# Softmax of differential attention: the maxima of both score maps by one vector instruction

## What is computed

```python
def diff_attend(q, keys, values, mask, lam):
    s = jnp.concatenate([jnp.einsum("bqhmd,bkhmd->bhmqk", q, k, preferred_element_type=jnp.float32)
                         for k in keys], axis=-1) * (B_HD ** -0.5)
    s = jnp.where(mask, s, jnp.finfo(jnp.float32).min)
    p = jax.nn.softmax(s, axis=-1)
    a = p[:, :, 0] - lam * p[:, :, 1]
    ...
    return sum(jnp.einsum("bhqk,bkhe->bqhe", a_i, v_i.astype(jnp.float32))
               for a_i, v_i in zip(parts, values))
```

## Time and profile before

| | |
|---|---|
| median of 3 runs | 3868.49 us (3865.95 to 3873.62) |
| profiled execution, its own time | 3872.43 us |
| its span, first to last instruction | 3870.3 us |
| PE busy | 3542.8 us (92%) |
| DVE busy | 1532.7 us (40%) |
| ACT busy | 1100.9 us (28%) |
| POOL busy | 787.7 us (20%) |

### The profile page before, as it was taken

One profiled execution on the slowest core, in us unless ns is written; L12 is line 12 of the kernel. 1 busy time (PEld: TensorE's weight loads), 2 busy tenths in 40 slices (PEclk: granted clock), 3 DMA queues, 4 the chain that ended last, 5 costly groups with the idle time before them and its releaser, 6 DMA issues. The chain is left out here.

```text
span 3870.3 us, 56244 instructions
## 1 busy us (share of the span) xinstructions
PE 3542.8 (92%) x21831; PEld 3369.7 (87%) x21831; DVE 1532.7 (40%) x2332; ACT 1100.9 (28%) x1863; POOL 787.7 (20%) x477
## 2 busy tenths in 40 slices
PE   5888888888897899999999998888898999999998
PEld 5888788788787899999999877777777999999998
DVE  2544534534433542222223344444445622222222
ACT  2332333332332221111112334434444221111111
POOL 1213313213212131111111311111110231111110
PEclk7999899899898899999999989999999999999999
DMA  2010000001000111111111111111111111111111
GB/s 87 17 29 18 24 27 19 24 18 28 24 18 18 39 44 44 45 44 45 44 44 44 59 46 51 51 51 51 51 50 34 44 44 46 44 48 43 46 44 63
DMA packets 254676, 155.75 MB, mean 40 GB/s; under 512 B 9521, under 2 KB 251587, under 8 KB 254403
## 3 DMA queue, kind: packets, MB, share of 16 engines
q1 hardware_dynamic: 254426, 152.14, 13.5%
HBM read 133.69 MB, written 18.42 MB: 39 GB/s over the span
## 5 line engine op out<-in xcount | busy, mean ns | idle before, releaser
L210 PE MATMUL ps<-x_hi,w_hi 128*128 128x364 f32 x2880 | 693.3, 349 | 30.6 <-DVE conv_in_sample L1090 17.5
L210 PE MATMUL ps<-x_hi,w_lo 128*128 128x364 f32 x2880 | 644.6, 332 | 0.0
L210 PE MATMUL ps<-x_lo,w_hi 128*128 128x364 f32 x2880 | 644.4, 332 | 0.0
L210 PEld LDWEIGHTS ps<-x_hi,w_hi 128*128 128x128 f32 x2880 | 502.6, 192 | 68.1 <-issue 21.5
L210 PEld LDWEIGHTS ps<-x_lo,w_hi 128*128 128x128 f32 x2880 | 509.5, 191 | 0.0
L210 PEld LDWEIGHTS ps<-x_hi,w_lo 128*128 128x128 f32 x2880 | 509.1, 191 | 0.0
L200 DVE TENSOR_TENSOR w_lo<-w_raw,w_hi 128x1024 fp32r<-128x1024 f32 x200 | 282.8, 1414 | 509.3 <-ACT w_hi L196 509.2
L196 ACT ACTIVATE w_hi<-w_raw 128x1024 fp32r<-128x1024 f32 x200 | 211.7, 1059 | 833.7 <-PE ps L210 616.0
L190 POOL TENSOR_TENSOR w_raw<-w_raw,params 128x1024 f32<-128x1024 f32 x120 | 232.9, 1944 | 891.0 <-DMA w_raw<-in_w_in_a 408.1
L210 PE MATMUL ps<-hidden_hi,w_lo 128*128 128x364 f32 x1536 | 338.3, 328 | 0.0
L210 PE MATMUL ps<-hidden_lo,w_hi 128*128 128x364 f32 x1536 | 337.7, 328 | 0.0
(11 more groups left out here) (321 smaller groups left out, 4967.0 us busy)
## 6 DMA issues: line engine op xcount, KB each, us to landing
w_raw<-in_w_up SPq DMA_DIRECT2D x64, 512.0 KB, 3.9
w_raw<-in_w_down SPq DMA_DIRECT2D x64, 512.0 KB, 3.4
w_raw<-in_w_in_a SPq DMA_DIRECT2D x32, 512.0 KB, 4.1
w_raw<-in_w_kv SPq DMA_DIRECT2D x16, 512.0 KB, 4.0
cache_pages<-in_cache_k SPq DMA_DIRECT2D x128, 64.0 KB, 1.9
cache_pages<-in_cache_v SPq DMA_DIRECT2D x128, 64.0 KB, 1.9
x_in<-in_x_prompt SPq DMA_DIRECT2D x8, 512.0 KB, 4.3
state_sample<-in_state_delta SPq DMA_DIRECT2D x8, 512.0 KB, 4.0
```

What stands on the lines that cost most here:

```text
L210: mm = nc.tensor.matmul(PS[:, bank + g, 0:GRP], wt, x[:, k, g * GRP:(g + 1) * GRP], start=(k == 0 and t == 0), stop=(k == chunks - 1 and t ...
```

## The change

One reduce now takes the maxima of both maps: it reads a view of PSUM with two rows per partition (`score_rows`) and writes two numbers, and one instruction negates both. The exponentials remain two instructions, and each waits for the joint maximum. The scores give one signal for a step, after the last mask matmul, where each map had its own. So that the two rows lie at an even distance, the short steps (0 to 3) put their maps in banks 0 and 1 or 2 and 3, where they had 0 and 2 or 1 and 3; the long steps keep their banks.

```diff
-    b_s = Steps(nc, "scores", 2 * NT)
-    b_mx = Steps(nc, "score_max", 4 * NT)
+    b_s = Steps(nc, "scores", NT)
+    b_mx = Steps(nc, "score_max", 2 * NT)
...
     def score_bank(i, m):
-        return 2 * m + (i % 2 if i < 4 else 0)
+        return 2 * (i % 2) + m if i < 4 else 2 * m
...
+    def score_rows(i):
+        b = score_bank(i, 0)
+        return PS[:, b:b + 2, 0:(i + 1) * P] if i < 4 else \
+            PS[:, 0:4, :].rearrange("p (m b) c -> p m (b c)", m=2)[:, :, 0:(i + 1) * P]
...
                 mm = nc.tensor.matmul(PS[:, score_bank(i, m) + i // 4, d], IDH[map_rows(m), part, :],
                                       MDH[map_rows(m), part, :], start=False, stop=part == 1)
-                if part == 1:
-                    mm.then_inc(b_s.sem, 1)
+        mm.then_inc(b_s.sem, 1)
...
                 for m in range(2):
-                    act.wait_ge(b_mx.sem, b_mx.at(h, 4 * i + 2 * m + 2))
+                    act.wait_ge(b_mx.sem, b_mx.at(h, 2 * i + 2))
...
             def maxima(i):
-                for m in range(2):
-                    dve.wait_ge(b_s.sem, b_s.at(h, 2 * i + m + 1))
-                    nc.vector.tensor_reduce(SC[:, i, 0, m:m + 1], score_row(i, m), AX.X, ALU.max).then_inc(b_mx.sem, 1)
-                    dve.wait_ge(b_mx.sem, b_mx.at(h, 4 * i + 2 * m + 1))
-                    nc.vector.tensor_scalar(SC[:, i, 1, m:m + 1], SC[:, i, 0, m:m + 1], -1.0, None, ALU.mult
-                                            ).then_inc(b_mx.sem, 1)
+                dve.wait_ge(b_s.sem, b_s.at(h, i + 1))
+                nc.vector.tensor_reduce(SC[:, i, 0, :], score_rows(i), AX.X, ALU.max).then_inc(b_mx.sem, 1)
+                dve.wait_ge(b_mx.sem, b_mx.at(h, 2 * i + 1))
+                nc.vector.tensor_scalar(SC[:, i, 1, :], SC[:, i, 0, :], -1.0, None, ALU.mult).then_inc(b_mx.sem, 1)
```

## The result

The change makes the kernel slower: 3920.86 us median (3918.33 to 3924.78, 4 runs) where the kernel before, run beside it, took 3868.08 (3865.95 to 3873.62, 4 runs). The ratio is 1.0135, 95% interval [1.0118, 1.0153], or +52.8 us. The forecast was 3903 in a range up to 3918: the direction was right, and the time lies 3 us above the upper end. The profiled execution took 3918.33 with a span of 3916.2, which is 45.9 us above the span of before.

A forecast was written before the change was run, and what follows sets the result against it. Bound: each softmax step's ring of VectorE, ScalarE and PE, without slack, delaying PE and the end. Lost overlap 30.7 + joint score signal 0.8 + POOL holds 3 = 34.5 us on 3868.5, giving 3903; range 3893 to 3918.

The forecast's parts named there:

- The lost cover: Softmax steps 1 to 7: map 0's exp no longer overlaps map 1's maximum; one exp lost less fixed costs, 30.7 us.
- The rivals that said not slower: VectorE's instructions bound (3850, chance 0.03); delay absorbed by PE or load (3868, 0.04); two-row maximum at one row's price (3864, 0.03).
- The holds: POOL's weight-slab scaling (L190) in the softmax loops holds VectorE's instructions in more heads than three: +3 us, bounds -5 and +8.
- the mix that the prediction names: Head 2's VectorE mix at 2449.31, expected to slide 1.4 us to 2450.7, behind POOL's scaling start at 2450.63.
- The upper bound of +8: Upper bound for added delay from POOL's slab scaling: all seven heads with such a slab are held.
- The one signal of the scores: First maximum also waits for map 1's last mask matmul, step 1 above all: 0.8 us, bounds 0 and 2.
- the banks: Steps alternate between two PSUM bank pairs as before, with PE's order and waits the same: nothing.
- PE's clock: Longer gaps before the scores may bring the lower granted clock to six more heads: 8.5 us, 3912, chance 0.20.
- the projection stretches stay unchanged: Sign of being right: softmax stretches grow some 4 to 6 us a head, while projections behind them keep their length.
- the rival: More than the sum: PE's lower clock at step 6 in six more heads, 6 x 1.42 = 8.5 us, 3912; chance 0.20.
- 0.50 in steps 4 to 6 of most heads: Granted-clock sign in the softmax loops that would show the forecast wrong and the lower-clock rival (chance 0.20) right.
- gaps of 1.41 us at each step: Argument against the lower-clock rival: head 2's PE idles this long before scores at each step without the clock dropping.

The follow-up runs named there:

- the filler: Changed kernel with POOL's slab scaling late, plus two extra unused PE matmuls ahead of the transposes of steps 1 and 2 each; 3904.67 us, ratio 1.0091.
- the pair without holds: Kernel before and changed kernel, each with POOL's slab scaling waiting until the running softmax loop's mixes are done; 3862.73 us and 3916.08 us.

## Why the prediction was wrong in its sum, and what it had right

**The lost cover, 30.7 us: right.** Step 6 of head 2 was forecast at exp 0 after 2.24 and exp 1 after 3.25 us and came at 2.26 and 3.26; the idle time before the reciprocal was to be 2.1 and is 2.15; the fused reduce at 896 columns a map was to be near 2.0 us and is 2.02, on the line drawn through the single reduces. Step for step, the reciprocal comes later by 0.29 us (step 1) to 0.92 (step 7) in the written-out heads and by 0.19 to 0.83 in the looped ones; the steps 1 to 7 of all heads make 30.9. That it is the cover was shown by the kernel in which only the wait was moved: +1.00 us in that step, one exp, and +48.0 in sum, where 8 x 5.55 plus one exp of step 0 a head is about 47.

**The rivals that said not slower: wrong, as forecast.** The Trainium skill, "VectorE: DVE Perf Modes", "Rules for kernel authors", wants the operation count minimized. The runs disagree for this case in the form of the change (128 fewer, +52.8 us) and agree for the negation in the reduce (128 fewer, -7.9 us): the count is worth something only where the instructions that go were not what lets another engine begin.

**The holds, +3: right in size, with some luck.** They went from 4.9 to 8.8 us, +3.9, and as forecast they were spread over more heads: one in each of heads 0 to 6, 0.6 to 1.6 us, where three heads had one. The scaling began where it had, 19 to 24 us after a head's first maximum. But VectorE slid by step 4's wait as well, which was not in the sum, and the mix that the prediction names was held in one head only; in five it was step 4's combination, in one a negation. The upper bound of +8 was too high by its own numbers: seven holds of 1.64 us are 11.5, which is 6.6 more than the three of before. Nor are the holds worth their length: with the scaling moved, the two kernels gained 3.4 and 4.8 us, 1.4 apart, and without holds the late scores of the changed kernel rose from 17.0 to 21.6.

**The one signal of the scores, 0.8, and the banks, 0.** The banks ran alone at no cost. The signal has no experiment of its own; the waits of step 1, where it was put, are 6.8 us before and 6.1 after. At the 17 waits of after the last two mask matmuls begin 6 to 40 ns apart, 0.3 us in all, and more than that the signal cannot have cost there.

**PE's clock: the step that failed.** The sum had it at nothing, with the sentence that the projection stretches stay unchanged; only the rival gave it a price, 8.5 us, put it on step 6 and gave it a chance of 0.20. The runs show that the term is not nothing: the lower clock struck step 4 in all eight heads (9.5 us of waiting, 1.1 before) and the stretch behind each loop (gaps +4.4), while step 6 waited for 1.4 us in all, less than the 2.8 of before. In the profiled pair the late scores and the gaps are 10.6 us, most of the miss in that pair (45.9 for 34.5). By the prediction's own sign, 0.50 in steps 4 to 6 of most heads, it is this rival that came true; that its price comes near is luck, since it was worked out for another step. Without holds step 6 was struck too. The error in the reasoning was to ask whether the gaps at one step of head 2 bring the low clock there, and to find that gaps of 1.41 us at each step do not; PE's gaps before the scores of steps 4 to 7 there are 0.95 to 1.41 us, so 1.41 is only the longest. The trace of before had a low stretch in every head in the first half of the loop, and one at its end; both were there to be seen, and I should have asked where they move when the loop gets longer and emptier, and who waits there.

The medians differ by 52.8, 7 us more than the two profiled executions. The mean granted clock that each run carries says which way this goes: the profiled execution after had 0.944, the three others 0.940 to 0.941 and 3920 to 3925 us; before it had 0.948 and was itself 4 us above its median. No trace of those other runs exists, so where they lose it is not shown, and these 7 us of the miss stay open.

That late scores and longer gaps come from the clock was tested by the filler, in the pair without holds: PE does more, the mean granted clock goes from 0.941 to 0.949, step 4's wait is gone, and the time falls by 11.4 us to 3904.7. That this lies near the forecast of 3903 confirms no number: without holds the kernel before takes 3862.7, and with the chain's 31.5 us that would be 3894. Most of the 10 us in between are late scores at step 6 and gaps, or lie outside the loops: the filler took the lower clock off step 4, but not out of the loop. The Trainium skill, "TensorE: Matmul & The Clock Gate", "What's actually happening", says that activity releases the throttle; the run agrees.

## What to carry to other kernels

Before two small instructions are merged into one, look at who starts on the first result: here the overlap was worth one whole exp a step, and the merge gave back only fixed costs. A loop that makes TensorE wait longer has a second price, the stretch at the lower clock: look where it lies now, where it will lie when the loop is longer, and whether anybody waits for scores there. Where the instruction count itself is to be cut, cut it within one engine's chain (here the negation in the reduce), so that nothing that others wait for moves back.

## What the runs showed of the hardware that was not expected

A two-element negation was held by POOL like a large instruction. Head 3 after, in the timeline:

```profile
2564.03 1.90 POOL L190 TENSOR_TENSOR w_raw<-w_raw,params 128x1024 f32<-128x1024 f32 x1 [29.64 <-DMA w_raw<-in_w_kv]
2564.16 1.80 DVE L2135 TENSOR_SCALAR softmax_scalars<-softmax_scalars 128x2 f32<-128x2 f32 x1
```

It lasted 1.80 us, where 0.17 is usual. The kernel with two reduces and one negation has such a hold too, 1.27 us, in the same head. The one-element negation of before ran through POOL's scaling of head 2, which lasted from 2450.63 to 2452.53, without delay. (That scaling began 0.02 us before map 1's maximum, and not in the middle of it, as the prediction has it.) The negation:

```profile
2451.64 0.15 DVE L2132 TENSOR_SCALAR softmax_scalars<-softmax_scalars 128x1 f32<-128x1 f32 x1
```

The Trainium skill, "SBUF — State Buffer", "Who interferes with whom", counts tensor_scalar among the operations that can take the port pair which VectorE shares with GpSimd, if its operands allow a mode with two ports. "VectorE: DVE Perf Modes" of the Trainium skill, "What auto-detection actually checks", makes that mode depend on a single source and the destination in SBUF whose outermost dimensions other than one are both even or equal. The trace agrees, with two elements held and one not; that it applies to two elements as well was the surprise.

A reduce over two rows goes by the total of its columns: 692 ns for 2 x 256, 1218 for 2 x 512, 2284 for 2 x 1024, the same 1218 that a single row of 1024 takes.
